# Eight PSUM banks in turn in the preparation of a hybrid decoder layer, the compression's first layers issued between other products, and the decay rate moved behind the recurrence gates

## What is computed

```python
u = h @ w_in        # x_lru, y_lru, q_dn, kv_dn, k_pe, q_n, kc, vc, ks, vs, kw, vw, g_n
a_out = rg_lru(causal_conv(x_lru), ...) * gelu(y_lru)
#   rg_lru: r, i = sigmoid(block_diag(x, wa)), sigmoid(block_diag(x, wx))
#           log_a = -8 * r * softplus(-lam);  h = scan(exp(log_a), sqrt(1 - a^2) * i * x)
b_out = mla_group(...)      # 6 heads, causal softmax over 512 keys, latent q and kv
kc = compress(rope(kc_in)); vc = compress(vc_in)   # gelu(windows of 32 tokens @ w1) @ w2: 31 rows
c_out = g0 * attend(q, kc, vc) + g1 * attend(q, selected ks, vs) + g2 * attend(q, window kw, vw)
x = x + concat(a_out, b_out, c_out) @ w_out
```

## Time and profile before

| | us |
|---|---|
| median of 3 runs (1520.47 to 1526.72) | 1522.11 |
| the profiled execution | 1521.48 |
| its span (first to last instruction) | 1519.6 |
| PE busy | 1378.6 (91% of the span) |
| DVE busy | 947.5 (62%) |
| ACT busy | 698.8 (46%) |
| share of the chain that ended last: PE, DVE, ACT | 74%, 12%, 7% |

### The profile page before, as it was taken

How to read it: one execution, slowest core, us unless ns; L and a number is a source line. 1 busy time by engine, 2 the same in 40 slices (tenths; PEclk the granted TensorE clock), 3 DMA queues, 4 the chain that set the end, 5 groups by cost and what they waited for, 6 DMA issues and landing times.

```text
span 1519.6 us, 27286 instructions
## 1 busy us (share of the span) xinstructions
PE 1378.6 (91%) x11566; PEld 911.9 (60%) x11624; DVE 947.5 (62%) x1423; ACT 698.8 (46%) x1078; POOL 90.6 (6%) x85
## 2 busy tenths in 40 slices
PE   3998799989999999998997998879999999999992
PEld 1346455434444444443355554369999999999982
DVE  5864777465540344117845775477677788888886
ACT  3342676243220232104345663165555566666662
POOL 0010200230000000130000000400000000000002
PEclk9998899989999999999999799979999999999997
DMA  5420582215420342005220000147678788889985
GB/s 198 179 84 28 167 293 81 95 45 199 161 83 1 126 164 110 0 23 208 69 70 26 3 1 12 44 174 284 223 265 290 282 315 320 316 332 346 341 297 181
DMA packets 37143, 244.65 MB, mean 161 GB/s; under 512 B 5224, under 2 KB 6632, under 8 KB 22560
## 3 DMA queue, kind: packets, MB, share of 16 engines
q1 hardware_dynamic: 29632, 216.62, 39.0%
q0 software_dynamic: 6816, 25.69, 5.2%
q10 hardware_dynamic: 576, 0.64, 0.1%
HBM read 214.40 MB, written 26.44 MB: 158 GB/s over the span
## 4 chain that ended last, share of the span: by engine, by line
PE 74%; DVE 12%; ACT 7%; issue 4%; DMA 1%; POOL 0%; another core or an unknown queue 0%; ACTq 0%; SPq 0%; DVEq 0%; POOLq 0%
PE bank L965 18%; PE bank L966 17%; PE bank L967 16%; PE bank L1146 3%; ACT arena L677 3%; PE bank L1172 2%; PE bank L1200 2%; DVE arena L797 2%; PE bank L570 2%; PE bank L569 2%; PE bank L571 2%; PE bank L535 2%; DVE arena L1536 1%; ACT arena L1463 1%; DVE small L1812 1%
## 5 line engine op out<-in xcount | busy, mean ns | idle before, releaser
L797 DVE SCALAR_TENSOR_TENSOR arena<-arena 128x3072 f16<-128x3072 f32 x86 | 288.8, 3358 | 77.6 <-ACT arena L677 77.3
L677 ACT ACTIVATE arena<-arena 128x3072 f16<-128x3072 f32 x86 | 237.0, 2756 | 0.2
L965 PE MATMUL bank<-arena 128*128 128x512 bf16 (+4 forms) x880 | 210.6, 262 | 8.1 <-DVE arena L1600 4.4
L966 PE MATMUL bank<-arena 128*128 128x512 f16 (+4 forms) x880 | 210.4, 262 | 0.0
L967 PE MATMUL bank<-arena 128*128 128x208 bf16 (+4 forms) x870 | 206.5, 260 | 0.0
L965 PE MATMUL bank<-hh,wring_hi 128*128 128x512 bf16 (+1 forms) x338 | 129.9, 384 | 14.7 <-DVE hl L1550 12.9
L569 PE MATMUL bank<-arena 128*128 128x128 bf16 (+5 forms) x704 | 139.9, 229 | 1.2 <-DVE arena L830 1.2
L965 PE MATMUL bank<-hh,arena 128*128 128x512 bf16 x350 | 133.5, 382 | 7.6 <-DVE hl L1550 6.5
L571 PE MATMUL bank<-arena 128*128 128x128 bf16 (+5 forms) x704 | 139.9, 229 | 0.0
L570 PE MATMUL bank<-arena 128*128 128x128 f16 (+5 forms) x704 | 139.9, 229 | 0.0
L966 PE MATMUL bank<-hl,wring_hi 128*128 128x512 f16 x352 | 135.2, 384 | 4.7 <-DVE hl L1563 3.9
(11 more groups left out here) (287 smaller groups left out, 2564.6 us busy)
## 6 DMA issues: line engine op xcount, KB each, us to landing
arena<-in_ew SPq DMA_DIRECT2D x86, 1536.0 KB, 8.4
arena<-in_dw SPq DMA_DIRECT2D x22, 1536.0 KB, 6.4
wstage<-in_w_chunk SPq DMA_DIRECT2D x44, 512.0 KB, 3.5
expert_results<-iota POOLq DMA_DIRECT2D x9, 2048.0 KB, 21.9
arena<-in_cmp_w SPq DMA_DIRECT2D x2, 2048.0 KB, 9.7
expert_results<-wstage SPq DMA_DIRECT2D x7, 512.0 KB
arena<-in_w_tok SPq DMA_DIRECT2D x2, 1096.0 KB, 6.1
xT<-in_x SPq DMA_DIRECT2D x4, 512.0 KB, 6.8
```

The lines of the kernel that those rows point to most:

```text
L677: act.activation(ew_hi_[:, G % EP, :], ew[:, G % ES, :], ACT.Copy, scale=SW).then_inc(M["hi_ready"], 1)
L797: dve.scalar_tensor_tensor(out=ew_lo_[:, G % EP, :], in0=ew[:, G % ES, :], scalar=SW, in1=ew_hi_[:, G % EP, :], op0=ALU.mult, op1=ALU.subt ...
L965: pe.matmul(out, w_hi, x_hi, start=first, stop=False)
L966: pe.matmul(out, w_hi, x_lo, start=False, stop=False)
```

## The change

Three edits to how the preparation is issued; no arithmetic changes.

1. `take` hands out eight banks in turn, and waits for the last reader of that very bank (`last_reader`). In a layer the count starts at bank 1, so that it ends with bank 7. The general waits at the end of the preparation go: attention's score, transpose and output banks each wait for their own last reader on first use (`emptied`). The output projection starts at bank 0 and uses eight as well; the router's jobs stay with four.
2. `hid` is no longer a step for PE: `hidden_beside` yields its 16 products, two in front of each three products of feat 10 (hidden layer 0) and tok 1 (hidden layer 1). ACT's and DVE's parts move with the list.
3. In `PREPARE`, `lam` moves from in front of tok 1 to behind `lru_gates` 1; `hid` 0 from behind feat 9 to feat 10, `cmp` 0 from feat 10 to feat 11, `cmp` 1 from tok 1 to behind tok 2, uv 2 and 3 come right behind the rotation of q 2.

```diff
-    ("feat", 9), ("rope", ("kw", 0)), ("hid", 0), ("wtok", 0), ("uk", 2),
-    ("feat", 10), ("rope", ("q", 0)), ("cmp", 0), ("lru_gates", 0), ("lru_gates", 1),
-    ("feat", 11), ("rope", ("q", 1)), ("win", 1), ("uv", 0), ("uv", 1),
-    ("tok", 0), ("rope", ("q", 2)), ("hid", 1), ("uv", 2), ("uv", 3),
-    ("lam", 0), ("tok", 1), ("cmp", 1), ("cmp_scores", 0), ("cmp_max", 0),
-    ("tok", 2), ("lru_decay", 0),
+    ("feat", 9), ("rope", ("kw", 0)), ("wtok", 0), ("uk", 2),
+    ("feat", 10), ("hid", 0), ("rope", ("q", 0)), ("lru_gates", 0), ("lru_gates", 1), ("lam", 0),
+    ("feat", 11), ("cmp", 0), ("rope", ("q", 1)), ("win", 1), ("uv", 0), ("uv", 1),
+    ("tok", 0), ("rope", ("q", 2)), ("uv", 2), ("uv", 3),
+    ("tok", 1), ("hid", 1), ("cmp_scores", 0), ("cmp_max", 0),
+    ("tok", 2), ("cmp", 1), ("lru_decay", 0),
...
+HID_BESIDE = {("feat", 10): 0, ("tok", 1): 1}
...
-        RING = 4
+        RING = 8
...
-            def take(job, reader):
+            place = [0]
-                n = len(jobs)
-                if n >= RING:
-                    pe.wait_ge(*ready(*jobs[n - RING]))
-                jobs.append(reader)
-                ring_of[job] = n % RING
-                return bank[n % RING]
+            def take(job, reader, banks=RING):
+                at = place[0] % banks
+                place[0] = at + 1
+                if at in last_reader:
+                    pe.wait_ge(*ready(*last_reader[at]))
+                last_reader[at] = reader
+                ring_of[job] = at
+                return bank[at]
+            def emptied(*banks):
+                for at in banks:
+                    pe.wait_ge(*ready(*last_reader[at]))
...
+                def hidden_beside(step, which):
+                    s = HID_BESIDE.get((step, which))
+                    if s is None:
+                        return
+                    b = take(("hid", l, s), ("hid", l, s))
+                    pe.wait_ge(*ready("cmp_w", l))
+                    pe.wait_ge(*ready("win", l, s))
+                    for lp in range(LP):
+                        mm = pe.matmul(b[:, 0:2 * NCMP], cw1[:, s, lp, :], win[:, lp, :, :],
+                                       start=(lp == 0), stop=(lp == LP - 1))
+                        if lp == LP - 1:
+                            mm.then_inc(*signal("hid_mm", l, s))
+                        yield
...
+                    hidden = hidden_beside("feat", j)
                     for k in range(KC):
+                        for _ in zip(range(LP // KC), hidden):
+                            pass
...
-                for job in jobs[-RING:]:
-                    pe.wait_ge(*ready(*job))
+                assert place[0] == RING
...
+                        if n < 4:
+                            emptied((n + 2) % 4)
```

More of the change, by code:

```diff
@@ L358, in trunk @@
         ring_of = {}
-        jobs = []
+        last_reader = {}
         dense_sems = ("gate_mm", "up_mm", "silu", "product", "act_ready", "down_mm", "y_added", "hi_ready", "lo_ready",
@@ L389, in dense @@
         def dense(pe, product):
-            for job in jobs[-RING:]:
-                pe.wait_ge(*ready(*job))
+            for reader in last_reader.values():
+                pe.wait_ge(*ready(*reader))
             with pe.Fori(0, HALVES) as e:
@@ L430, in route @@
         def route(pe, take, product):
-            b = take(("router",), ("lg",))
+            b = take(("router",), ("lg",), 4)
             pe.wait_ge(*ready("router_lo"))
@@ L455, in turn_half @@
                 for i in range(TT):
-                    b = take((family, i), (family, i))[:, :].bitcast(dtype)
+                    b = take((family, i), (family, i), 4)[:, :].bitcast(dtype)
                     for k in range(KC):
@@ L459, in turn_half @@
                     mm.then_inc(*signal(family + "_mm", i))
-            b = take(("count",), ("places",))
+            b = take(("count",), ("places",), 4)
             pe.wait_ge(*ready("sel"))
@@ L974, in _ @@
             for l in range(DEPTH):
+                place[0] = 1
                 if l == 0:
@@ L1017, in tok @@
                     t = slice(i * P, (i + 1) * P)
+                    hidden = hidden_beside("tok", i)
                     for k in range(KC):
+                        for _ in zip(range(LP // KC), hidden):
+                            pass
                         mm = product(b[:, 0:TOKW], hh[:, k, t], hl[:, k, t], wtok_hi[:, k, :], wtok_lo[:, k, :],
@@ L1061, in uv @@
                               stop=True).then_inc(*signal("uv_mm", l, i))
[L1063 to L1071, removed]
                 def compress_out(s):
@@ L1116, in _ @@
                 part = {"feat": feat, "tok": tok, "rope": rope_turn, "norm": latent_sum, "uq": uq,
-                        "uk": uk, "uv": uv, "hid": compress_hidden, "cmp": compress_out, "cmp_scores": cmp_scores,
+                        "uk": uk, "uv": uv, "cmp": compress_out, "cmp_scores": cmp_scores,
                         "lru_gates": lru_gates, "turn_cmp": turn_cmp}
@@ L1167, in turn @@
                         pe.wait_ge(*ready("pn", l, n))
+                        if n < 2:
+                            emptied(4 + n)
                         if n >= 2:
@@ L1181, in values @@
                     if opens and kb == 0:
+                        if u < 2 * 2:
+                            emptied(6 + chunk % 2)
                         before = {5: None, 6: None, 7: 5, 2: 6, 3: 7, 4: 2}[chunk]
@@ L1213, in _ @@
                     values(NU - 1, kb)
+                place[0] = 0
                 for m in range(KC):
```

## The result

The changed kernel takes 1510.57 us (median of 6 runs, 1506.58 to 1515.59), against 1526.66 for the kernel before beside it (6 runs, 1520.47 to 1528.17). The ratio is 0.991, 95% interval 0.9886 to 0.9934. A second series gave 0.9919 (0.989 to 0.9949). So it is faster by about 14 us by the first ratio and 12 by the second. The median lies inside the range on record. The profiled execution, the slowest of the six, took 1515.59 (span 1513.7), only 5.9 us less than the one before, and lies outside. Where the 16 us that were forecast are, and why one execution shows 6 of them, is the question of what follows.

The account below looks back on a forecast made before the run. PE bounds the kernel (busy 91% of the span, 74% of the chain). Gains of 8.4 us in layer 0 and 7.5 in layer 1, 15.9 off 1521.5, give 1505.6, rounded to 1506 with half of 0.6; range 1500 to 1512.5.

Parts of the forecast that it names:

- Part 1: Eight banks in the preparation: rotation waits go, 2.66 us per layer, and score-bank waits of 1.66 and 2.81; attention's start zero.
- Part 2: Hidden-layer products between those of feat 10 and tok 1: no saving, bounds -0.9 to +1.6 us per hidden layer.
- The rival of an emptied array: Each f32/16-bit change empties PE, 64 in all; gain gone from 0.25 us each, 1536 us at 0.47; chance 0.04.
- Part 3: Decay rate behind the gates: DVE's chain from 118.3, window ready at 128.8, PE waits 1.3 us at tok 1.
- which I expect gone because big products now stand between the small ones: Low clock around layer 0's hidden layer 1, over 132.7 to 139.4 us: expected to vanish, saving 3.3 us.
- Rival 1: Low clock stays behind the scores or at attention's start, 1.5 to 2 us per layer: 1509.5 us; chance 0.25.
- Scores and behind: Scores take twice 1.75 us without waits, end at 138.9; transposes at 151.9; layer 0 gains 8.4 us, layer 1 7.5.
- Behind that point both layers run as before (0 for the start of attention, as above): After the transposes of the probabilities, in both layers: no change in time, zero gain at attention's start.
- The rule on table loads: Trainium skill's 1.38 us drain per ACT table switch: window 4.1 us later per layer, 1514 us; forecast used 1.28 per load.

Follow-up runs that it names:

- e11: The changed kernel run once more with no edit, for a second profile; median 1509.73 us, ratio 0.9919 against the kernel before.
- e5: The changed kernel with nine unused 128x512 products in front of PE's wait for window 1; 1506.36 us, ratio 0.9878 against the kernel before.
- e4: The changed kernel with the decay rate moved once more, behind the rotation of q 2; 1500.26 us, ratio 0.9862 against the kernel before.
- e1: The kernel before with only the ring of eight banks, old list and hidden layers as steps; 1514.27 us, ratio 0.994.
- e8: The kernel before with only the decay rate moved behind the second recurrence gates; 1513.97 us, ratio 0.9948.
- e6: The changed kernel with twenty unused products in attention's first wait for ACT; 1504.27 us, ratio 0.9865 against the kernel before.
- e12: The changed kernel with the decay rate behind the rotation of q 2 and hidden layers as their own steps; 1504.61 us, ratio 0.9876 against before.

## Why the prediction was right or wrong

**Size and sign.** Forecast 1506 and -16 us; measured 1510.6, and -16.1 by the medians of one series, -14 by the ratio. 4.5 us of the difference in the absolute time are the reference: 1522.11 was a median of three runs, of six it is 1526.66. That the medians, and e11's profile most of all (1505.45 us where 1505.6 was worked out), come so near is partly luck. In e11 the two stretches gained 19.7 us and not 15.9, 1.8 came where nothing was forecast, and from the transposes of layer 1 to the end it took 702.8 us (1503.7 - 800.89) where before took 697.2 (1519.6 - 822.36): 5.6 us lost, also where nothing was forecast.

**Part 1 held.** Both rotation waits and the one for a score bank are gone, the first attention scores don't wait, and the wait behind them is 4.73 us where 4.7 was forecast; counting zero for it was right (13.85 us from the transposes to n = 4, before and after).

**Part 2.** Zero was too cautious by 0.4 us per hidden layer. Four hidden instructions beside three products of tok take 128.94 - 128.20 = 0.74 us, of which 0.35 are tok's; that leaves 0.39 where alone they take 0.44. In e11 tok 1 with hidden 1 took 6.1 where 6.5 was forecast. The rival of an emptied array (0.25 us and more per change) has nothing for it.

**Part 3 held almost to the digit, and its consequence was mis-sized.** DVE in the changed kernel, layer 0:

```profile
118.06 0.17 DVE L1675 TENSOR_SCALAR small<-small 128x2 f32<-128x2 f32 x1 [3.11 <-ACT small L1368]
...
123.33 1.22 DVE L1583 SCALAR_TENSOR_TENSOR wring_lo<-wstage,wring_hi 128x1024 f16<-128x1024 f32 x1
...
126.64 1.89 DVE L1766 TENSOR_TENSOR arena<-arena 128x496 f32<-128x496 f32 x2
```

The chain starts at 118.06 (forecast 118.3) and the window is ready 1.9 us behind 126.64, in time for hidden 1 at 128.67 (forecast 128.8). But PE came to it at 126.7 and not at 127.5, through hidden 0's 0.4 us and, it seems, changes from step to step that I had rounded up. So the wait was 2.0, not 1.3 us.

**The first step that failed** is the sentence "which I expect gone because big products now stand between the small ones" (3.3 us of layer 0, and the same risk in layer 1). In the profiled execution the clock fell beside tok 1, in front of its second group of big products, in both layers: 6.8 us of low clock in each stretch, where none was forecast. All sixteen layers counted above have big products between the small ones; the stretch was long only in layers with the wait in front, and there not always. I had the row for it (0.90 us and a low clock in layer 0, the same wait and none in layer 1), forecast that this wait would grow, and still put the low clock down to narrow products alone. Rival 1 had the low clock behind the scores or at attention's start, not at tok 1, and priced it at 1.5 to 2 us per layer; it was 3.3.

**Scores and behind.** I took 3.5 us for the scores; they took about 3.0 (48 instructions in a row from 133.47). From the scores' start to the transposes it was 149.08 - 133.47 = 15.6 us (forecast 16.5). So without a low clock the stretch gains 10.3 and 9.4 us, 2 more per layer than forecast, and with it 7.0 and 6.1, 1.4 less. Of the 10 us that the profiled execution missed the forecast by, that is 2.8.

**The second step that failed**, and the larger one, is "Behind that point both layers run as before (0 for the start of attention, as above)". It is 6.6 us of the 10. In the changed kernel's profile layer 1's attention, from n = 4 to the norm behind the output projection, took 148.5 us where before it took 144.1: low stretches from 822 to 829 and from 836 to 850 us with the 3.53 us wait for DVE between them. That and 2 us in the experts, which also began with a longer low stretch, is how 12.5 us at the transposes of layer 1 became 5.9 at the end. It was no accident of one execution: e11 and e5 lost 4.3 and 4.4 us in layer 1 as well, and none in layer 0 (143.8 and 143.7 against 145.2 before).

Over the six runs of the changed kernel time and mean granted clock go together: 1506.58 at 0.966, 1509.86 to 1510.64 at 0.964, 1513.86 at 0.962, 1515.59 at 0.961. 0.005 of clock is 1% of 1510 us at half speed, 15 us, and costs half of that, 7.6; the runs differ by 9.0. In e11 the six runs go from 1505.45 at 0.967 to 1514.34 at 0.961 and 1514.94 at 0.963.

**The rule on table loads.** ACT loaded three tables in front of the decay rate's exponential, and DVE got it at 118.06 where 1.28 us per load gave 118.3. The last of the three and the exponential, in ACT's order of time:

```profile
116.53 1.28 ACT L1368 ACT_TABLE_LOAD   x1
117.83 0.20 ACT L1368 ACTIVATE small<-small 128x2 f32<-128x2 f32 x1
```

The Trainium skill's drain (ScalarE: Activation LUTs, "What ACT_TABLE_LOAD costs"), 1.38 us more per load, would have made it 4.1 us later; the trace doesn't agree, and the measurement decides: behind each of the three loads the activation starts 0.01 to 0.02 us after the load's end.

## What to carry to other kernels

A ring of banks that is too short and a long chain of tiny operations in front of a reader look alike in the waits; ask of each wait what else stands in the releasing engine's queue, and move that. A move is best placed where the engine idles and nobody needs it for a while: one place further on (e4) brought 7 us by the ratios on top of the 14. Before you read a short stretch, ask the clock in it: e1's and e8's seem to say that the decay rate gives more than the ring, and at one clock it is the other way about. When products are put beside others, see which of them waits for what, or the wide ones inherit the narrow ones' wait.

## What the runs showed of the hardware

The same program, with the same 1.98 us wait at the same place, had the lower clock behind it in one profile and not in the next; 3.3 us in each of two layers hang on it. The two profiled executions of the changed kernel were 10 us apart, 1515.59 and 1505.45, and these two layers are 6.6 of them. So a gain of 1% is to be read from medians of many runs, and from short stretches whose clock is the same.

In the stretch of the preparation, where PE was busy for 94 to 99% of the time (before, changed, e8, e4), each us at 1.2 GHz cost 0.5 us: layers of one list with 0 and 6.8 us of it, or 3.4 and 6.8, agree within 0.2 us once half is taken off. In attention's first pair of heads, where DVE ends last, it cost less: in layer 1 DVE let PE go on 13.3 us behind n = 4 after 7 us at the lower clock (changed) and after 14 (e4), and 12.2 us behind it after 3.4 (e6).

A long low stretch doesn't need a wait in front of it. In e12 the clock fell while 31-column products ran right behind 62-column ones, in both layers and for 6.8 us each, and PE counted as busy throughout (7.00 of 7.00 us).
